# A planned order of work: ScalarE waits for a nearly ready piece rather than begin a split, and the sliding heads' products lie in one stretch

## What is computed

```python
h = rms_norm(x, norm_pre[l]); u = h @ w_in[l]
oa = diff_attention(...)                     # 4 heads, two maps each
qm = rms_norm(b_q, q_norm) @ mla_w_qb[l]     # latents expanded: 8 heads of 96
kvm = rms_norm(b_kv, kv_norm) @ mla_w_kvb[l]
ob = mla_attention(...)
oc = sliding_window_attention(c_q, c_k, c_v, sinks[l], rel_bias)   # 8 heads, 2 of keys
y = (gates[:, :, 0] * ((oa * silu(a_z)) @ w_br_a[l])
     + gates[:, :, 1] * ((ob * silu(b_z)) @ w_br_b[l])
     + gates[:, :, 2] * ((oc * silu(c_z)) @ w_br_c[l]))
x = x + rms_norm(y @ w_out[l], norm_post[l])
x = x + sigmoid(x @ w_ple_gate[l]) * (p[l] @ w_ple_proj[l])
```

## Time and profile before

| | us |
|---|---|
| median of 3 runs (lowest, highest) | 1910.88 (1909.26, 1911.4) |
| profiled execution, its own time | 1908.38 |
| its span | 1906.5 |
| TensorE busy | 1865.8 |
| GpSimd busy | 1516.2 |
| ScalarE busy | 945.2 |
| VectorE busy | 798.1 |

### The profile page before, as it was taken

How to read it: one execution, slowest core, us unless ns; L and a number is a source line. 1 busy time by engine, 2 the same in 40 slices (tenths; PEclk the granted TensorE clock), 3 DMA queues, 4 the chain that set the end, 5 groups by cost and what they waited for, 6 DMA issues and landing times.

```text
span 1906.5 us, 27403 instructions
## 1 busy us (share of the span) xinstructions
PE 1865.8 (98%) x9610; PEld 1529.7 (80%) x9610; DVE 798.1 (42%) x1933; ACT 945.2 (50%) x1501; POOL 1516.2 (80%) x1330
## 2 busy tenths in 40 slices
PE   8999999999999999999999999999999999999999
PEld 7878888877888887788887778887887887788877
DVE  6774110456111245411056641106857344455534
ACT  4564444454444445444435544434656654555743
POOL 7768979885897977797987779797686887777785
PEclk9999999999999999999999999999999999999999
DMA  8445656555666554465655456655564564556453
GB/s 292 137 146 178 187 164 223 179 176 145 184 193 214 188 172 149 144 188 164 223 150 157 152 166 187 208 169 174 178 182 122 161 209 152 162 170 178 130 173 111
DMA packets 184558, 330.54 MB, mean 173 GB/s; under 512 B 12221, under 2 KB 44521, under 8 KB 184425
## 3 DMA queue, kind: packets, MB, share of 16 engines
q1 hardware_dynamic: 176512, 323.21, 55.0%
q10 hardware_dynamic: 7912, 5.59, 1.0%
HBM read 325.35 MB, written 3.41 MB: 172 GB/s over the span
## 4 chain that ended last, share of the span: by engine, by line
PE 84%; POOL 6%; DVE 4%; DMA 3%; ACT 2%; issue 1%; SPq 0%; DVEq 0%; ACTq 0%
PE acc L1419 24%; PE acc L1420 23%; PE acc L1426 21%; POOL w_lo L1185 6%; PE tps L1366 4%; PE acc L1441 2%; PE acc L1422 2%; PE ops L1483 2%; PE tps L1459 2%; DMA raw<-in_w_down 1%; PE acc L1390 1%; PE acc L1392 1%; PE acc L1391 1%; DMA raw<-in_w_mem_kv 1%; PE ops L1378 1%
## 5 line engine op out<-in xcount | busy, mean ns | idle before, releaser
L1185 POOL TENSOR_TENSOR w_lo<-raw,w_hi 128x512 fp32r<-128x512 f32 (+2 forms) x1242 | 1475.3, 1225 | 349.9 <-ACT w_hi L1213 348.7
L1213 ACT CAST w_hi<-raw 128x1024 fp32r<-128x1024 f32 (+3 forms) x624 | 615.6, 991 | 745.3 <-PE acc L1426 567.2
L1419 PE MATMUL acc<-w_hi,xT_hi 128*128 128x512 f32 (+1 forms) x1808 | 687.1, 384 | 4.9 <-ACT U L1247 2.9
L1420 PE MATMUL acc<-w_lo,xT_hi 128*128 128x512 f32 (+1 forms) x1808 | 666.6, 372 | 0.0
L1426 PE MATMUL acc<-w_hi,xT_lo 128*128 128x512 f32 (+2 forms) x1744 | 505.2, 371 | 0.0
L1419 PEld LDWEIGHTS acc<-w_hi,xT_hi 128*128 128x128 f32 x1808 | 341.4, 189 | 74.6 <-issue 15.2
L1420 PEld LDWEIGHTS acc<-w_lo,xT_hi 128*128 128x128 f32 x1808 | 342.2, 189 | 52.4
L1426 PEld LDWEIGHTS acc<-w_hi,xT_lo 128*128 128x128 f32 x1744 | 317.8, 189 | 58.2 <-DVE xT_lo L1696 1.1
L1756 DVE TENSOR_TENSOR H<-G,acc 128x512 f32<-128x512 f32 (+1 forms) x48 | 30.9, 643 | 335.5 <-PE acc L1426 335.5
L1419 PE MATMUL acc<-w_hi,hT_hi 128*128 128x512 f32 x352 | 139.5, 396 | 3.6 <-POOL w_lo L1185 3.4
L1420 PE MATMUL acc<-w_lo,hT_hi 128*128 128x512 f32 x352 | 137.2, 390 | 0.0
(11 more groups left out here) (210 smaller groups left out, 1993.5 us busy)
## 6 DMA issues: line engine op xcount, KB each, us to landing
raw<-in_w_gate_up SPq DMA_DIRECT2D x160, 512.0 KB, 3.9
raw<-in_w_in SPq DMA_DIRECT2D x104, 512.0 KB, 3.8
raw<-in_w_down SPq DMA_DIRECT2D x88, 512.0 KB, 3.7
raw<-in_w_out SPq DMA_DIRECT2D x48, 512.0 KB, 3.6
raw<-in_w_in_a SPq DMA_DIRECT2D x32, 512.0 KB, 3.6
raw<-in_w_in_b SPq DMA_DIRECT2D x20, 512.0 KB, 3.7
raw<-in_w_mem_kv SPq DMA_DIRECT2D x16, 512.0 KB, 4.2
raw<-in_w_gate_up SPq DMA_DIRECT2D x32, 256.0 KB, 2.8
```

Source lines behind the costliest of these rows:

```text
L1185: ins = nc.gpsimd.tensor_tensor(w_lo[:, r, i, 0:ch.width], raw[:, r, i, 0:ch.width], w_hi[:, slot, i, 0:ch.width].bitcast(F32), ALU.subtract)
L1213: nc.scalar.copy(w_hi[:, u.u % SPLIT, 0:u.nk, 0:u.chunk.width], raw[:, u.u % RAW, 0:u.nk, 0:u.chunk.width]).then_inc(S["hi_ready"], 1)
L1419: nc.tensor.matmul(o, hi[:, tok], wh, start=first_k, stop=False)
L1420: ins = nc.tensor.matmul(o, hi[:, tok], wl, start=False, stop=False)
```

## The change

There are two parts. In `arrange`, every ScalarE task that is not a split gets `ahead = 600` (ns), and a few VectorE tasks of row tile 0 (the layer norms', the `rms_post` norm's and `ple_add`'s) get 1500. When the scheduler has chosen a task without `ahead`, it looks through the ready tasks of the same engine, and takes instead the first one with `ahead` that needs no PSUM room and can start less than `min(ahead, cost of the chosen task)` after the chosen one could. In the second block, the sliding heads' first 512 columns are multiplied ahead of their last 256, so both lie before the expansions.

```diff
+LEADS = ("ple_add", "layer_norm", "rms_post")
...
         self.prio = prio
+        self.ahead = 600 if eng == "ACT" and kind != "split" else 0
         self.lat = lat
...
             assert first is not None, [(k.kind, k.it) for t in ready.values() for k in t][:8]
+            k = first[1]
+            if not k.ahead:
+                for other in ready[k.eng]:
+                    at = max(other.at, clock[k.eng])
+                    if other.ahead and other.room is None and at < first[0][0] + min(other.ahead, k.cost):
+                        first = ((at,), other)
+                        break
             k = first[1]
...
     def stage(self, cost, fn, fed, prio=1, **kw):
-        return self.task("DVE", "stage", Stage(fn, fed, **kw), cost, "stage", fed, prio=prio)
+        one = self.task("DVE", "stage", Stage(fn, fed, **kw), cost, "stage", fed, prio=prio)
+        if fn in LEADS and kw.get("t") == 0:
+            one.ahead = 1500
+        return one
...
             first = p.task("DVE", "stage", Stage(fn + "_scale", fed[t], **st), scale, None, [*fed[t], *taken], prio=t - 1 if fn == "rms_pre" else 0)
+            if fn in LEADS and t == 0:
+                first.ahead = 1500
...
-        swc = copy(sw, 512, [(C_CQ + 512, 256)])
+        swc = copy(sw, 0, [(C_CQ, 512), (C_CQ + 512, 256)])
...
         turned_k = [p.stage(500, "latent_keys", [latent[t], *gone], t=t, src=low, dst=keys) for t in range(T)]
-        swc = copy(sw, 0, [(C_CQ, 512)]) + swc
```

## The result

| | before | after |
|---|---|---|
| median of 4 runs each (lowest, highest), us | 1910.38 (1909.26, 1911.4) | 1918.99 (1918.68, 1922.61) |
| ratio, 95% interval | | 1.0049 [1.0038, 1.0061] |
| profiled execution: its time, its span | 1908.38, 1906.5 | 1918.68, 1916.7 |
| TensorE busy, idle | 1865.8, 40.7 | 1868.5, 48.2 |

The change costs 8.6 us by the medians (7.3 to 11.7 by the interval) and 10.2 us by the spans of the two profiled executions. That is slower, and outside the range. The sign belongs to the slower rival.

What follows compares the result with a forecast made beforehand. The prediction took TensorE, busy 1865.8 of 1906.5 us, as the bound. Its terms −2.0 + 0 + 0 + 0 gave −2.0 us: 1906.4 for the profiled execution, 1908.9 for the median, range 1903.5 to 1916.0 us.

Steps and rivals of the forecast that it cites:

- the slower rival: Latent heads' stretch: gate sigmoids fall among exponentials, table loads become TensorE waits; 6.2 less 2.0, +4.2, 1915.1 us; chance 0.20.
- What bounds the kernel: TensorE busy 1865.8 of 1906.5 us, so any new order could win at most 40.7 us.
- The two waits behind a split: Exponentials near 1062 and 1668 us stand behind a ScalarE split; putting them first saves 0.93 and 1.05, −2.0 us.
- the 1.05: Saving at the second place, near 1666 us: mixed maps come 1.05 us earlier without the split in front.
- What the rule adds: Splits held behind pieces put ahead on ScalarE: 1.2 us each, hidden by idle time; 0, bounds 0 and +4.8.
- +4.8 for four: Upper bound for splits held up in the four w_down stretches, 1.2 us in each.
- The lead marks: VectorE's first-row-tile norms and adds put ahead: no wait arises or goes; 0, bounds −0.67 and +1.5 us.
- The moved stretch: Sliding heads' first 512 columns ahead of the latents' expansions: 0; bounds −0.53 per layer, above the slower rival's waits.
- The cover of 22.5 us: Latent heads' last value product leads the branch by 22.5 us; moved later by 10.9, it still leads by 11.6.
- the 2.0 us of credit: The forecast's saving of 2.0 us from two waits behind splits, subtracted from the slower rival's 6.2 us.
- The price of a load: ScalarE table load: 1.28 us by the rows, about 2.66 by the skill page, making the slower rival 5.5 us dearer.

Runs made afterwards that it cites:

- m3: The kernel before with ScalarE's 600 ns rule alone, no VectorE lead marks and no moved stretch: 1914.91 us, ratio 1.0026.
- n17: The whole change, with the 600 ns mark taken off ScalarE's sigmoid and silu evictions only: 1912.97 us, ratio 1.0016.
- m4: The kernel before with VectorE's lead marks alone, no rule on ScalarE and no moved stretch: 1911.38 us, ratio 1.0009.
- m2: The kernel before with both planner rules (ScalarE's and the lead marks), without the moved stretch: 1913.32 us, ratio 1.0019.
- m1: The kernel before with the moved stretch alone, no rule in the planner: 1909.09 us, ratio 0.9999.
- n14: The whole change with all marks, the planner's clock charging 1283 ns for each ScalarE table load: 1904.40 us, ratio 0.9971.
- t5: The kernel before with sigmoid gates computed by tanh, 22 table loads in place of 41: 1904.28 us, ratio 0.9980.
- n12: The whole change with all marks dropped from the first block's tasks: 1919.24 us, ratio 1.0054.
- t6: The whole change with sigmoid gates computed by tanh, 26 table loads in place of 43: 1909.77 us, ratio 1.0005.
- x8: The kernel before with mixed maps cut to the scaling, one SBUF input in place of two, the addition left out: 1907.55 us, ratio 0.9996.

## Why the prediction was wrong

**What bounds the kernel.** Right that an order could win no more than the 40.7 us of idle time. Wrong in the sign of the room: nothing bounded what an order could lose in a stretch that stood at 0.55 us of idle, and it lost there.

**The two waits behind a split.** For the earlier trace rows it was right: the maxima now end at 1064.61, the exponentials begin at 1064.64, and TensorE has no wait near 1066. The later layers of the first block lost two more waits that I had not found, 0.82 us each at layer norms, and got three new ones for rounded attention outputs (0.94, 0.58 and 0.94 us, at 770.23, 1084.66 and 1091.06). For the earlier trace rows it was wrong, and the 1.05 never came. The same order stands 5.94 us later, split in front, and the wait is as long as before (timeline of TensorE after):
```profile
1680.28 0.55 PE L1473 MATMUL tps<-ident,L 128*128 128x128 f32 x3 [1.75 <-DVE L L2026]
```
Its pair of maps took 2.81 us beside GpSimd's low halves; that was in the chain too, and I had counted the split alone.

**What the rule adds, taken as 0.** This is the step that failed. I priced the rule by what it does to splits, and that price was about right: one wait for `w_lo` at the head of a w_down stretch grew from 0.41 to 1.24 us, where the bound was +4.8 for four, and the splits still idle 681.2 us. I didn't price which piece it puts forward. The rule takes the first marked one, and a sigmoid of the gate counts like an exponential, by a clock that doesn't know its load. ScalarE's rule alone cost 5.0 us (m3): its stage of the first differential attention is 2.2 us longer, its latent stages 1.8 and 1.6. Beside the move the two latent stages lost 4.5 and 4.3, and they lost nothing once silu and sigmoid had no mark (n17: +0.25 and +0.10).

**The lead marks.** m4 measured +1.7 us by its ratio, with an interval from 0 to 3.4, where I took 0 and the bounds were −0.67 and +1.5; that doesn't settle it. What its profiled execution has more lies in the first block. Beside ScalarE's rule the marks gained 1.3 (m2 against m3), which is within the intervals. One of their effects showed where I had looked for it: the wait at the second layer's start is 1.43 us after, where the earlier trace rows has 2.62.

**The moved stretch, taken as 0.** Right for the move alone, 0.9999 (m1), and wrong as a term of a sum: with both rules it cost 5.7 us. The cover of 22.5 us that I worked out was for the last value product and the branch; the waits came in the steps before, at each exponential and sigmoid. My bound was "the waits of the slower rival", and there the case was priced.

**The slower rival** was the right mechanism at the right place: gate sigmoids among the exponentials of the latent heads, with a load each way. It forecast 6.2 us of new waits; TensorE's idle time rose by 3.1 and 3.3 us in the two stages, 6.4. That the sizes meet is in part luck. The rival's waits were to be for the gate's banks, and those (`tmp`) rose by 0.9 us per stage; the others stand at scaled probabilities (0.65 and 0.97), at copies by VectorE (0.3) and at an eviction into U (0.2). From its +4.2 to the +10.2 of the spans it lacked four things: the 2.0 us of credit that it took from the forecast, 2.5 us by which the two stages grew beyond their idle time (4.5 + 4.3 less 6.4), in which TensorE counts as busy longer for the same products, 2.0 in the stage of the differential attention and 1.5 in the first block; 2.0 came back around the second layer's start, 0.7 of it with the clock. I gave it 0.20 because TensorE "has no wait at all there". That was read too widely: the window of the earlier trace rows ends at 1770, and the kernel before has two waits for `tmp` in each of these stages (0.53 and 0.39; 0.55 and 0.39, at 1779.28 and 1818.40). ScalarE was busy for 32.97 of 43 us there, and three loads more in 38 us, with the sigmoids ahead of the exponentials, were enough.

**The price of a load.** The Trainium skill, page "ScalarE: Activation LUTs", section "What ACT_TABLE_LOAD costs", has 2.66 us per switch, load and drain; the rows have 1.28, with the next activation 0.01 us behind the load (1463.80 + 1.28, then 1465.09) and the one before it ending at 1463.77. The rule of the same page, section "Table sets: the hidden batching unit", to batch activations by set would have been the better guide here. By its figure the slower rival would have been 5.5 us dearer, 1920.6; the measured 1918.99 doesn't bear the figure out, since what lies above the rival's 1915.1 comes from the other places named above.

**What stays open.** Why the kernel with the rules and without the move is 3 us slower than before even with the charge; why the stage of the first differential attention is 2 us longer with the rules; and which of its many moves gave n14 its gain. By idle time its profiled execution has 11.4 us less than that of the whole change: 6.9 in the two latent stages, 4.7 in the two of the differential attention.

## What to carry to other kernels

In a list scheduler, first make its clock right: a cost that depends on what the engine did before (a table load) must be charged in the order in which it falls. The same two rules and the same move cost 8.6 us by a clock that left 1.28 us loads out, and gained 5.5 by one that had them. It is no guarantee: the rules without the move stayed 3 us slower than before by the right clock too.
Edits to such a planner don't add: the moved stretch was worth +5.7, 0, −3.4 and, with the rules and the charge, −8.6 us, by what stood around it. Measure the combination, and don't price it as a sum of parts.
A stage with no wait at the bounding engine isn't a safe one: ask how full its neighbour is, and what one more switch there would do.

## What the runs showed of the hardware

A table load took 1.28 us in every kernel, and the next activation started at once. What one costs the program depends on its place: 0.24 us on average over the 19 that t5 took out. Among the exponentials of the latent heads the whole change has 8 loads in 38 us against 5, and doing the gates by tanh took 2.4 us per layer off what the change costs there.

The same pair of VectorE instructions, 128x128 in and out of SBUF, took 0.75 us with GpSimd idle and up to 2.86 with GpSimd at its low halves; with one input 0.55 and up to 2.68. The excess of 2.1 for two instructions is about one low half each (4.38 us for 4, above). That GpSimd is the cause is argued, as said above.

TensorE's granted clock fell to half, 1.2 GHz, for 3.5 us behind a wait of 1.80 us in the kernel after (from about 1346.7). In n12 and t6 the same wait of 1.80 us at the same place was followed by the full clock.

The Trainium skill, page "GPSIMD Engine Reference", section "1. Specifications", has the SBUF interfaces shared with VectorE, in contention where VectorE has two inputs in SBUF or runs in a two-port mode. By the page "VectorE: DVE Perf Modes", section "What auto-detection actually checks", one source and a destination in SBUF, with outermost dimensions that are even or equal, put an instruction into a two-port mode. So x8 took away the one condition and met the other, and its miss agrees with the two pages read together; I had read only the first half of the rule.
